# Feed-forward outputs taken from the sum ahead of its layer norm, with mean and factor applied afterwards

## The chip, the cores and the metric

The kernel runs on one core of a Trainium2 chip. The metric is the device time of one execution in microseconds (us), median of the runs shown. TensorE multiplies (PE, and PEld for its weight loads), VectorE (DVE) and ScalarE (ACT) prepare operands and read results, SyncE (SP) issues the loads of weights.

## What is computed

The program runs two transformer blocks; only the end of the second is touched. There the mixer's output is added to the stream and normed, and a gated feed-forward follows (sizes: 256 tokens, D_MODEL 1024, D_FF 2816):

```python
def layer_norm(x, g, b):
    mu = jnp.mean(xf, axis=-1, keepdims=True)
    var = jnp.mean(jnp.square(xf - mu), axis=-1, keepdims=True)
    y = (xf - mu) * lax.rsqrt(var + LN_EPS)
    return (y * g + b).astype(x.dtype)

x = layer_norm(alpha * x + mix, ln1_g[l], ln1_b[l])
ff = (jax.nn.silu(x @ w_ffn_gate) * (x @ w_ffn_up)) @ w_ffn_down
x = layer_norm(alpha * x + ff, ln2_g[l], ln2_b[l])
```

## The kernel before

**Operands.** Everything is fp32 split in two: each operand has a high part (rounded to the matmul's fp32r) and a low part (the rest), and each product is three matmuls, high by high, low by high, high by low. Weights stream in chunks of 128x1024 through a ring of four raw buffers (`raw`, loaded by SP); ScalarE rounds each into `whi` (`highs`), VectorE subtracts to get `wlo` (`lows`), and both of these are rings of five. `highs` and `lows` stand by hand in each engine's program and convert up to 4 (ScalarE) or 3 (VectorE) chunks ahead of the one named.

**Layout.** Activations lie transposed: 8 tiles (`k`) of 128 features by 256 tokens. `XT` holds the stream, `hx` its high and low parts. The first 256 columns of `hx` are the feed-forward's input; the other 256 columns later hold its inner values (`K.fh`, `K.fl`).

**Up to the norm.** Eight outputs `("wo", m)` of 24 matmuls each end the mixer. For each, VectorE adds the stream (`x1`), and VectorE and ScalarE build running sums and squares. The norm itself (`ln1`) takes these steps in turn: eight one-column matmuls sum over partitions (`ln1_sums`, "s1" and "s2"), VectorE makes mean and factor of them and puts them on a diagonal, one matmul each (`ln1_spread`, "m" and "r") spreads them over all partitions, and then, tile by tile, VectorE subtracts the mean (`x1_centre`), multiplies (`x3t`), ScalarE adds the bias and rounds (`x3h`, then `x3`), and VectorE takes the low part (`x3_low`). `keep(n)` puts matmuls on zeros in between, whose results nobody reads.

**Feed-forward.** There are 22 steps `f` (KF); step `f` needs the gate output `("fg", f)`, the up output `("up", f)`, then Silu, the product, its split, and the down matmuls `down(f)` into four held PSUM banks. The first four outputs (fg and up of steps 0 and 1) run side by side in `lin_many`, tile by tile as `x3` comes; later ones run one by one in `lin_wide`. Steps 0 to 3 also carry four groups of transposes of the normed stream (`x3t`), for the residual. `down` of step f-3 stands after the outputs of step f.

**PSUM.** There are eight banks. `Psum.take` gives the bank that was taken longest ago and returns what must have happened to its last holder (`ps.give` says what); TensorE waits for that before the first matmul into it:

```python
        i = min(free, key=lambda i: (max(self.age[i:i + n]), i))
        ...
                out += self.freed.get(self.holder[j], [])
```

**Order on VectorE and ScalarE.** Each is one in-order list. In the feed-forward's loop over `m`, VectorE's first instructions of a step are `lows(("fg", m))` and `lows(("up", m))`, and ScalarE's first is `highs(("fg", m))`. So the chunk of `fg 3` is converted by ScalarE at the start of m = 1, behind the last instruction of m = 0, which is the copy into `K.fh` (L1446), and by VectorE at the same place, behind the subtraction into `K.fl` (L2165).

Of the kernel before, what the change touches and what calls it, by code (L numbers as in the profile page):

```python
# [2482 lines left out]
```

## Time and profile before

| | |
|---|---|
| median of 3 runs | 894.1 us (892.78 to 896.55) |
| profiled execution, its own time | 894.56 us |
| its span in the profile | 892.8 us |
| TensorE busy | 872.5 us, 98% |
| VectorE busy | 627.1 us, 70% |
| ScalarE busy | 440.3 us, 49% |
| TensorE's granted clock, mean | 0.996 |

Matmuls are pipelined, so TensorE counts as busy in small pauses too; the start times of its instructions show where it really stands. Times below are microseconds from the span's start. "x4" after a row means four instructions in it; the bracket at a row's end gives the engine's idle time before it and who ended that.

### The profile page before, as it was taken

How to read it: one execution, taken by the hardware profiler on the slowest of the kernel's cores; microseconds unless marked ns; L12 is line 12 of the kernel's file. 1: busy time of each engine (PE TensorE's matmuls, PEld its weight loads, DVE VectorE, ACT ScalarE, POOL GpSimd, SP SyncE). 2: the span in 40 equal slices, each digit the busy share in tenths (PEclk: the TensorE clock that was granted, in tenths of full speed). 3: DMA queues.
4: the chain of work that ended last, by engine and by line, in shares of the span. 5: the costliest groups of instructions: out<-in, count | busy, mean ns of one | idle time of the engine just before them, and what ended most of it. 6: DMA issues, size and time to landing. Idle time of an engine off the chain costs nothing.

```text
span 892.8 us, 13280 instructions
## 1 busy us (share of the span) xinstructions
PE 872.5 (98%) x5324; PEld 709.2 (79%) x5324; DVE 627.1 (70%) x1252; ACT 440.3 (49%) x750; POOL 21.2 (2%) x16
## 2 busy tenths in 40 slices
PE   8999999999999999999999999999999999999996
PEld 4678477776687777877998888988999888888885
DVE  5532757594836759966699999978688775665666
ACT  3351515543723356555544444566554665555552
POOL 0000000000000000000002121100000000000000
PEclk9999999999999999999999999999999999999999
DMA  9784551100354033203556656441366365546541
GB/s 351 284 319 171 203 197 61 48 25 1 119 196 161 16 130 142 84 23 142 167 189 188 190 173 204 142 143 59 103 196 210 113 201 206 188 175 204 190 164 47
DMA packets 39997, 136.68 MB, mean 153 GB/s; under 512 B 4352, under 2 KB 4480, under 8 KB 39680
## 3 DMA queue, kind: packets, MB, share of 16 engines
q1 hardware_dynamic: 38928, 130.48, 42.8%
q10 hardware_dynamic: 1008, 5.36, 1.6%
q8 instruction: 42, 0.69, 0.3%
q14 instruction: 19, 0.16, 0.1%
HBM read 134.77 MB, written 1.05 MB: 152 GB/s over the span
## 4 chain that ended last, share of the span: by engine, by line
PE 68%; DVE 25%; ACT 3%; DMA 2%; issue 1%; SPq 0%; DVEq 0%; ACTq 0%
PE ps L414 8%; DVE wlo L1472 7%; PE ps L971 6%; DVE AF L1941 6%; PE ps L415 4%; PE ps L369 4%; PE ps L370 4%; PE ps L374 3%; PE ps L733 3%; PE ps L489 3%; PE ps L386 2%; DMA AF<-wmod 2%; PE ps L397 2%; PE ps L756 2%; PE ps L398 2%; PE ps L401 2%
## 5 line engine op out<-in xcount | busy, mean ns | idle before, releaser
L1472 DVE TENSOR_TENSOR wlo<-raw,whi 128x1024 fp32r<-128x1024 f32 (+2 forms) x204 | 231.6, 1158 | 34.4 <-ACT whi L1009 34.2
L1009 ACT ACTIVATE whi<-raw 128x1024 fp32r<-128x1024 f32 (+2 forms) x204 | 203.5, 1005 | 86.2 <-DMA raw<-wpack 45.8
L369 PE MATMUL ps<-hx,whi 128*128 128x256 f32 (+1 forms) x384 | 115.4, 300 | 0.3 <-ACT AF L1350 0.3
L414 PE MATMUL ps<-hx,whi 128*128 128x512 f32 x320 | 113.9, 398 | 0.0
L370 PE MATMUL ps<-hx,whi 128*128 128x256 f32 (+1 forms) x384 | 112.0, 292 | 0.0
L374 PE MATMUL ps<-hx,wlo 128*128 128x256 f32 (+1 forms) x332 | 96.9, 292 | 0.0
L415 PE MATMUL ps<-hx,wlo 128*128 128x256 f32 x320 | 89.8, 281 | 0.0
L369 PEld LDWEIGHTS ps<-hx,whi 128*128 128x128 f32 x384 | 73.3, 191 | 3.8 <-issue 2.3
L370 PEld LDWEIGHTS ps<-hx,whi 128*128 128x128 f32 x384 | 73.4, 191 | 2.0 <-issue 0.7
L459 PE MATMUL ps<-whi,hx 128*128 128x512 f32 (+1 forms) x192 | 71.7, 373 | 0.2 <-ACT acc L1078 0.2
L414 PEld LDWEIGHTS ps<-hx,whi 128*128 128x128 f32 x320 | 60.1, 188 | 14.6
L460 PE MATMUL ps<-wlo,hx 128*128 128x512 f32 (+1 forms) x192 | 70.8, 369 | 0.0
L461 PE MATMUL ps<-whi,hx 128*128 128x512 f32 (+1 forms) x192 | 70.7, 368 | 0.0
L374 PEld LDWEIGHTS ps<-hx,wlo 128*128 128x128 f32 x332 | 63.4, 191 | 1.1
L415 PEld LDWEIGHTS ps<-hx,wlo 128*128 128x128 f32 x320 | 60.4, 189 | 0.7
L1941 DVE SCALAR_TENSOR_TENSOR AF<-AF,cst 128x256 f32<-128x256 f32 x120 | 58.0, 529 | 0.4
L1827 DVE TENSOR_REDUCE AF<-ps 128x1 f32<-128x512 f32 (+1 forms) x48 | 28.7, 598 | 32.1 <-PE ps L733 32.1
L971 PE MATMUL ps<-whi,hx 128*128 128x512 f32 x176 | 50.5, 391 | 0.0
L1240 ACT ACTIVATE AF<-ps 128x512 f32<-128x512 f32 (+1 forms) x48 | 25.0, 523 | 42.9 <-PE ps L741 42.9
L733 PE MATMUL ps<-AF 96*128 96x512 f32 (+1 forms) x96 | 43.1, 530 | 0.4 <-DVE AF L1750 0.4
L1233 ACT ACTIVATE AF<-ps,AF 128x512 f32<-128x512 f32 (+1 forms) x48 | 29.5, 615 | 26.1 <-DVE AF L1827 25.6
L459 PEld LDWEIGHTS ps<-whi,hx 128*128 128x128 f32 x192 | 36.7, 191 | 5.8 <-ACT acc L1078 0.4
(293 smaller groups left out, 1667.2 us busy)
## 6 DMA issues: line engine op xcount, KB each, us to landing
raw<-wpack SPq DMA_DIRECT2D x178, 512.0 KB, 4.1
AF<-wmod SPq DMA_DIRECT2D x48, 512.0 KB, 6.0
raw<-wpack SPq DMA_DIRECT2D x24, 256.0 KB, 2.7
XT<-xin SPq DMA_DIRECT2D x4, 512.0 KB, 6.0
raw<-wpack SPq DMA_DIRECT2D x4, 432.0 KB, 4.9
uq<-wuq ACTq DMA_DIRECT2D x2, 768.0 KB, 5.4
cst<-cpack ACTq DMA_DIRECT2D x1, 1093.0 KB, 8.0
AF<-wukv ACTq DMA_DIRECT2D x2, 512.0 KB, 6.7
```

Of the source, the lines that this page charges most:

```text
L369: e.matmul(o, wh[:, b], xh(k), start=j == 0, stop=False, skip_group_check=True)
L370: e.matmul(o, wh[:, b], xl(k), start=False, stop=False, skip_group_check=True)
L374: e.matmul(o, wl[:, b], xh(k), start=False, stop=False, skip_group_check=True)
L414: e.matmul(ps.ap(key, 512).rearrange("p (s n) -> p s n", s=2), wh[:, b], K.hx[:, :, k, 0:256], start=k == 0, stop=False, skip_group_check= ...
L415: i = e.matmul(ps.ap(key, 256), wl[:, b], hh[:, k, 0:256], start=False, stop=k == KD - 1, skip_group_check=True)
L459: e.matmul(o, xh(k)[:, ts], wh[:, b], start=k == 0, stop=False, skip_group_check=True)
L460: e.matmul(o, xh(k)[:, ts], wl[:, b], start=False, stop=False, skip_group_check=True)
L461: i = e.matmul(o, xl(k)[:, ts], wh[:, b], start=False, stop=k == KD - 1, skip_group_check=True)
L971: i = e.matmul(ps.ap(("fd", t), 512, 512 * q), y[:, f % 8, x], w[:, 512 * q:512 * q + 512], start=f == 0 and y is K.fh and w is wh, stop=f ...
L1009: e.activation(W.hi(i), W.raw(i), ACT.Copy).then_inc(*HI.up(j))
L1472: e.tensor_tensor(W.lo(i), W.raw(i), W.hi(i), ALU.subtract).then_inc(*LO.up(j))
L1941: e.scalar_tensor_tensor(out=g.CV[:, m, :], in0=g.U[:, m, j:j + 256], scalar=w, in1=g.CV[:, m, :], op0=ALU.mult, op1=ALU.add).then_inc(*V. ...
```

## The change

The six outputs of steps 0, 1 and 2 (RAW = 3) no longer read the normed input. Their input is `K.rx`: the sum ahead of the norm times the norm's weight, as high and low parts, in the columns 256 to 511 of `hx`; two more columns (256 wide becomes 258) hold the norm's weight and bias themselves. So each output comes with two extra numbers per partition, by which VectorE turns it into what the normed input would have given: copy the two numbers, (mean row x first number + output), times the factor row, and the bias number enters in Silu's bias or in the product. The sums and spreads of the norm now stand between the matmuls of `lin_raw`, and the matmuls on zeros are gone. Mean and factor rows are copied out of PSUM by ScalarE. The normed stream is still made as before, for steps 3 and up and for the residual; the four groups of transposes move from steps 0 to 3 to steps 3 to 6.

```diff
@@ tensor_program
-    keep(1)
-    ln1_sums("s1", K.acc[:, 0:256], K.XT[:, 7, XC], V["x1sum", 6], V["x1", 7])
-    ln1_sums("s2", K.acc[:, 256:512], K.sq[:, 768:1024], V["sqadd", 6], A["x1sq", 7])
-    ln1_spread("m", 256)
-    keep(2)
-    ln1_spread("r", 0)
-    keep(2)
+    rh, rl, rw = (lambda k: K.rx[:, 0, k, :]), (lambda k: K.rx[:, 1, k, :]), (lambda k: V["xr", k])
...
+    def lin_raw(specs):
+        got = []
+        for key, wname, cols in specs:
+            free = ps.take(key)
+            got.append((weights(key, (wname, 0, tuple(range(KD)), cols), KD * P), free))
+        for k in range(KD):
+            b = slice(k * P, (k + 1) * P)
+            pe.wait_ge(A["gb"], A["xr", k], V["gb"], V["xr", k])
+            for (key, wname, cols), ((c, wh, wl), free) in zip(specs, got):
...
+            if k == 0:
+                ln1_sums("s1", K.acc[:, 0:256], K.XT[:, 7, XC], V["x1sum", 6], V["x1", 7])
+                ln1_sums("s2", K.acc[:, 256:512], K.sq[:, 768:1024], V["sqadd", 6], A["x1sq", 7])
+            if k == 1:
+                ln1_spread("m", 256)
+            if k == 2:
+                ln1_spread("r", 0)
@@ for f in range(KF)
-            lin_many([((nm, j), f"w_ffn_{w}_2", 0, (P * j, P), x2h, x2l, 256) for j in range(2) for nm, w in (("fg", "gate"), ("up", "up"))], lambda k: A["x3h", k], xt3)
-        elif f > 1:
-            lin_wide(("fg", f), "w_ffn_gate_2", cc, xt3)
-            lin_wide(("up", f), "w_ffn_up_2", cc, xt3)
-        if f < 4:
+            lin_raw([((nm, j), f"w_ffn_{w}_2", (P * j, P)) for j in range(2) for nm, w in (("fg", "gate"), ("up", "up"))])
+        elif 1 < f < RAW:
+            lin(("fg", f), "w_ffn_gate_2", 0, cc, range(KD), rh, rl, 258, rw)
+            lin(("up", f), "w_ffn_up_2", 0, cc, range(KD), rh, rl, 258, rw)
+        elif f >= RAW:
+            lin_wide(("fg", f), "w_ffn_gate_2", cc, xt3, ps.bank.get(("ln1", "s2")) if f == RAW else None)
+            lin_wide(("up", f), "w_ffn_up_2", cc, xt3, ps.bank.get(("ln1", "m")) if f == RAW else None)
+        if RAW <= f < RAW + 4:
@@ scalar_program
+    def raw_high(m):
+        ac.wait_ge(V["x1", m])
+        e.activation(K.rx[:, 0, m, 0:256], XT[:, m, XC], ACT.Copy, scale=C("l1g", m, 1)).then_inc(*A.up(("xr", m)))
...
+    highs(("up", 1), 1)
+    for what, z in (("m", 0), ("r", 256)):
+        ac.wait_ge(M["ln1", what])
+        e.activation(K.acc[:, z:z + 256], ps.ap(("ln1", what), 256), ACT.Copy).then_inc(*A.up(("ln1", what)))
...
+        if k == 4:
+            highs(("up", 1), 2)
...
-        ac.wait_ge(V["fu", m], M["fd", m - 8, 1] if m >= 8 else None)
+        ac.wait_ge(V["fu", m], M["fd", m - 8, 1] if m >= 8 else M["up", RAW - 1])
         e.activation(K.fh[:, m % 8, :], K.AF[:, 512 + z:768 + z], ACT.Copy).then_inc(*A.up(("f", m)))
@@ vector_program
+    def raw_low(m):
+        dv.wait_ge(A["xr", m])
+        e.scalar_tensor_tensor(out=K.rx[:, 1, m, 0:256], in0=XT[:, m, XC], scalar=C("l1g", m, 1), in1=K.rx[:, 0, m, 0:256], op0=ALU.mult, op1=ALU.subtract).then_inc(*V.up(("xr", m)))
...
     diagonal("r", 0, v)
+    lows(("up", 1), 1)
+    for m in range(5, 8):
+        raw_low(m)
     for k in range(2):
         x1_centre(k)
...
+        if k == 5:
+            lows(("up", 1), 2)
     x3_low(KD - 1)
-    lows(("up", 1), 1)
+    def normed(nm, m, y, dst):
+        sc = K.modrow[:, 4 * m + 2 * y:4 * m + 2 * y + 2]
+        dv.wait_ge(M[nm, m])
+        e.tensor_copy(sc, ps.ap((nm, m), 2, 256)).then_inc(*V.up())
+        dv.wait_ge(V.now(), A["ln1", "r"])
+        e.scalar_tensor_tensor(out=dst, in0=K.acc[:, 0:256], scalar=sc[:, 0:1], in1=ps.ap((nm, m), 256), op0=ALU.mult, op1=ALU.add).then_inc(*V.up())
+        ps.give((nm, m), V.now())
+        dv.wait_ge(V.now())
+        e.tensor_tensor(dst, dst, K.acc[:, 256:512], ALU.mult).then_inc(*V.up((nm + "n", m)))
...
+        if m < RAW:
+            normed("fg", m, 0, side[:, 0:256])
+            normed("up", m, 1, side[:, 256:512])
+            dv.wait_ge(A["fg", m], V.now())
+            e.scalar_tensor_tensor(out=h, in0=side[:, 256:512], scalar=K.modrow[:, 4 * m + 3:4 * m + 4], in1=K.AF[:, z:z + 256], op0=ALU.add, op1=ALU.mult).then_inc(*V.up(("fu", m)))
```

**Order on TensorE, where the mixer's last output ends.** Before, the sums (L943), the spreads (L948) and the matmuls on zeros (L524) stand here, and the first matmul of `lin_many` (L430) behind them:

```order
L372 MATMUL ps<-hx,wlo 128x256
L524 MATMUL ps<-zero 128x256 [waits dve_done]
L943 MATMUL ps<-cst,acc 128x1 [waits dve_done]
...
L943 MATMUL ps<-cst,wk 128x1
L948 MATMUL ps<-wk,cst 128x256 [waits dve_done]
L524 MATMUL ps<-zero 128x256 x2
L948 MATMUL ps<-wk,cst 128x256 [waits dve_done]
L524 MATMUL ps<-zero 128x256 x2
L430 MATMUL ps<-hx,whi 128x256 [waits w_low,act_done]
```

With the change, the place of the first filler is taken by `lin_raw`: L967 to L969 are its three matmuls for one tile and one output, L945 the sums, which stand behind twelve of them (the first of those, the last two and the sums are shown).

```order
L374 MATMUL ps<-hx,wlo 128x256
L967 MATMUL ps<-hx,whi 128x258 [waits w_low,act_done,dve_done]
...
L968 MATMUL ps<-hx,wlo 128x258
L969 MATMUL ps<-hx,whi 128x258
L945 MATMUL ps<-cst,acc 128x1 [waits dve_done]
L945 MATMUL ps<-cst,acc 128x1
...
L945 MATMUL ps<-cst,wk 128x1
L967 MATMUL ps<-hx,whi 128x258
```

So the sums moved behind the first tile of the four outputs, and nothing on zeros is left.

**Order on TensorE, fifth and sixth output.** These are the last matmuls of `lin_raw` and the first of `("fg", 2)`, L371, which is in `lin`:

```order
L968 MATMUL ps<-hx,wlo 128x258
L969 MATMUL ps<-hx,whi 128x258
L371 MATMUL ps<-hx,whi 128x258 [waits dve_done,w_low]
L372 MATMUL ps<-hx,whi 128x258
L376 MATMUL ps<-hx,wlo 128x258
```

L371 waits for VectorE as well as for its weights. Eight banks were taken since `("fg", 0)` took its own (four outputs, s1, s2, m, r), so `("fg", 2)` takes the bank of `("fg", 0)`, and what frees it is the second operation of `normed` for that output (L2201).

**Order on VectorE, end of the norm and step 0 of the feed-forward, before.** L2131 is `x3_low`, L2136 `x3t`, L1472 `lows`, L2153 the product of step 0, L2165 the low part of its result:

```order
L2136 SCALAR_TENSOR_TENSOR wk<-XT,cst,ps 128x256 [waits dve_done]
L2131 SCALAR_TENSOR_TENSOR hx<-wk,cst,hx 128x256 [waits act_done] x2
L1472 TENSOR_TENSOR wlo<-raw,whi 128x1024 [waits w_high]
L2153 TENSOR_TENSOR AF<-AF,ps 128x256 [waits act_done,mm_done]
L2165 TENSOR_TENSOR hx<-AF,hx 128x256 [waits act_done]
L1472 TENSOR_TENSOR wlo<-raw,whi 128x1024 [waits w_high] x2
```

And now, where L2186 is `x3t`, L2181 `x3_low`, L2199, L2201 and L2204 are `normed`, L2216 the product, L2227 the low part, L1511 `lows` (the last row is the chunk of fg 3):

```order
L2186 SCALAR_TENSOR_TENSOR wk<-XT,cst,acc 128x256 [waits dve_done]
L2181 SCALAR_TENSOR_TENSOR hx<-wk,cst,hx 128x256 [waits act_done] x2
L2199 COPY modrow<-ps 128x2 [waits mm_done]
L2201 SCALAR_TENSOR_TENSOR AF<-acc,modrow,ps 128x256 [waits dve_done]
L2204 TENSOR_TENSOR AF<-AF,acc 128x256 [waits dve_done]
L2199 COPY modrow<-ps 128x2 [waits mm_done]
L2201 SCALAR_TENSOR_TENSOR AF<-acc,modrow,ps 128x256 [waits dve_done]
L2204 TENSOR_TENSOR AF<-AF,acc 128x256 [waits dve_done]
L2216 SCALAR_TENSOR_TENSOR AF<-AF,modrow 128x256 [waits dve_done,act_done]
L2227 TENSOR_TENSOR hx<-AF,hx 128x256 [waits act_done]
L1511 TENSOR_TENSOR wlo<-raw,whi 128x1024 [waits w_high]
```

`normed` came in behind the last `x3_low`, and the conversion for fg 3 stands behind all of step 0.

**Order on ScalarE, from the norm's end to the chunk of fg 3, with the change.** L1457 is `x3`, L1475 Silu, L1485 the copy into `K.fh`, L1034 `highs`:

```order
L1462 ACTIVATE hx<-wk,cst 128x256 [waits dve_done]
L1457 ACTIVATE XT<-wk,cst 128x256 x2
L1475 ACT_TABLE_LOAD
L1475 ACTIVATE AF<-AF,modrow 128x256 [waits dve_done]
L1485 ACTIVATE hx<-AF 128x256 [waits mm_done,dve_done]
L1034 ACTIVATE whi<-raw 128x1024 [waits raw_in0]
```

L1485 waits for TensorE too, for the end of `("up", 2)`, because `K.fh` lies where the matmuls of steps 0 to 2 read. The conversion for fg 3 stands behind it.

## Rows read from the trace of the kernel before

**Rows 1.** The page: busy time, share of the span and instructions.

```profile
PE 872.5 (98%) x5324; PEld 709.2 (79%) x5324; DVE 627.1 (70%) x1252; ACT 440.3 (49%) x750; POOL 21.2 (2%) x16
```

**Rows 2.** Windows: length, PE, PEld, DVE, ACT, POOL busy (count), clock, DMA, GB/s.

```profile
691.40:697.87 6.47, 5.36 (x33) 4.30 (x32) 5.19 (x21) 0.93 (x2) 0.00 (x0) 1.00 0.67 246
697.87:709.30 11.43, 11.40 (x95) 11.43 (x96) 8.76 (x22) 9.59 (x19) 0.00 (x0) 1.00 0.04 5
725.00:733.40 8.40, 8.40 (x46) 7.17 (x45) 5.66 (x10) 5.35 (x10) 0.00 (x0) 1.00 0.62 213
```

**Rows 3.** Timeline, TensorE around the norm: start us, us, engine line.

```profile
691.53 0.59 PE L524 MATMUL ps<-zero 128*128 128x256 f32 x2
693.18 0.53 PEld L943 LDWEIGHTS ps<-cst,wk 128*128 128x128 f32 x4
693.63 0.30 PEld L948 LDWEIGHTS ps<-wk,cst 128*128 128x128 f32 x2
693.96 0.84 PEld L524 LDWEIGHTS ps<-zero 128*128 128x128 f32 x4
697.90 0.36 PE L430 MATMUL ps<-hx,whi 128*128 128x256 f32 x1 [0.34 <-ACT hx L1424]
```

**Rows 4.** Timeline of VectorE at the end of the mixer's output.

```profile
690.17 1.22 DVE L1472 TENSOR_TENSOR wlo<-raw,whi 128x1024 fp32r<-128x1024 f32 x1
691.73 0.42 DVE L2097 SCALAR_TENSOR_TENSOR XT<-XT,ps 128x256 f32<-128x256 f32 x1 [0.33 <-PE ps L372]
```

**Rows 5.** Timeline of VectorE in the norm.

```profile
693.94 0.16 DVE L2121 SCALAR_TENSOR_TENSOR nrm<-ps,nrm 128x2 f32<-128x2 f32 x1
695.85 0.75 DVE L2111 TENSOR_TENSOR XT<-XT,ps 128x256 f32<-128x256 f32 x2
696.73 0.48 DVE L2136 SCALAR_TENSOR_TENSOR wk<-XT,cst,ps 128x256 f32<-128x256 f32 x1
703.05 0.47 DVE L2136 SCALAR_TENSOR_TENSOR wk<-XT,cst,ps 128x256 f32<-128x256 f32 x1
704.91 0.48 DVE L2131 SCALAR_TENSOR_TENSOR hx<-wk,cst,hx 128x256 fp32r<-128x256 f32 x1 [0.20 <-ACT hx L1424]
```

**Rows 6.** Timeline of ScalarE in the norm.

```profile
701.74 0.50 ACT L1419 ACTIVATE XT<-wk,cst 128x256 f32<-128x256 f32 x1
```

**Rows 7.** Timeline of a feed-forward step, VectorE.

```profile
718.97 0.42 DVE L2163 TENSOR_TENSOR AF<-AF 128x256 f32<-128x256 f32 x1
719.88 0.42 DVE L2165 TENSOR_TENSOR hx<-AF,hx 128x256 fp32r<-128x256 f32 x1 [0.48 <-ACT hx L1446]
720.22 2.35 DVE L1472 TENSOR_TENSOR wlo<-raw,whi 128x1024 fp32r<-128x1024 f32 x2
```

**Rows 8.** Timeline of the same step, ScalarE.

```profile
719.43 0.42 ACT L1446 ACTIVATE hx<-AF 128x256 fp32r<-128x256 f32 x1 [0.94 <-DVE AF L2163]
719.75 0.58 ACT L1450 ACTIVATE AF<-ps 128x512 f32<-128x512 f32 x1
720.23 1.05 ACT L1009 ACTIVATE whi<-raw 128x1024 fp32r<-128x1024 f32 x1
```

**Rows 9.** Timeline, TensorE's weight loads at steps 3 to 5.

```profile
721.89 0.48 PEld L988 LDWEIGHTS ps<-cst,XT 128*128 128x128 f32 x4
722.34 0.30 PEld L971 LDWEIGHTS ps<-whi,hx 128*128 128x128 f32 x2
724.96 0.19 PEld L414 LDWEIGHTS ps<-hx,whi 128*128 128x128 f32 x1
733.35 0.19 PEld L414 LDWEIGHTS ps<-hx,whi 128*128 128x128 f32 x1
```

**Rows 10.** Windows, same columns: after one-column matmuls, and at the end.

```profile
84.00:86.00 2.00, 2.00 (x9) 2.00 (x10) 1.20 (x8) 0.00 (x0) 0.00 (x0) 0.50 0.00 0
86.00:88.00 2.00, 2.00 (x12) 2.00 (x12) 0.21 (x2) 0.00 (x0) 0.00 (x0) 0.66 0.00 0
888.00:890.00 2.00, 0.00 (x0) 0.00 (x0) 1.82 (x7) 0.00 (x0) 0.00 (x0) 0.87 0.00 0
```

More of the change, by code:

```diff
@@ L286 @@
 ITEMS2 = [(qb, h) for qb in range(2) for h in range(8)]
+RAW = 3
 LAST = KF - 4
@@ L404, in lin_rest, with lin_wide @@
         ps.drop(key)
-    def lin_wide(key, wname, cols, xw):
-        free = ps.take(key)
+    def lin_wide(key, wname, cols, xw, at=None):
+        free = ps.take(key, at=at)
         c, wh, wl = weights(key, (wname, 0, tuple(range(KD)), cols), KD * P)
@@ L948, in ln1_spread @@
         e.matmul(ps.ap(("ln1", what), 256), C("ones"), K.rs[:, z:z + 256], start=True, stop=True, skip_group_check=True).then_inc(*M.up(("ln1", what)))
-    keep(1)
-    ln1_sums("s1", K.acc[:, 0:256], K.XT[:, 7, XC], V["x1sum", 6], V["x1", 7])
-    ln1_sums("s2", K.acc[:, 256:512], K.sq[:, 768:1024], V["sqadd", 6], A["x1sq", 7])
-    ln1_spread("m", 256)
-    keep(2)
-    ln1_spread("r", 0)
-    keep(2)
-    xt3 = lambda k: V["x3", k]
+    rh, rl, rw = (lambda k: K.rx[:, 0, k, :]), (lambda k: K.rx[:, 1, k, :]), (lambda k: V["xr", k])
+    xt3 = lambda k: V["x3", k]
+    def lin_raw(specs):
[7 more added lines that the diff above has]
+            for (key, wname, cols), ((c, wh, wl), free) in zip(specs, got):
+                o = ps.ap(key, 258)
+                pe.wait_ge(*free)
+                e.matmul(o, wh[:, b], rh(k), start=k == 0, stop=False, skip_group_check=True)
+                e.matmul(o, wl[:, b], rh(k), start=False, stop=False, skip_group_check=True)
+                i = e.matmul(o, wh[:, b], rl(k), start=False, stop=k == KD - 1, skip_group_check=True)
+                if k == KD - 1:
+                    i.then_inc(*M.up(key))
+                    W.given[c] = M.now()
+            if k == 0:
[5 more added lines that the diff above has]
+                ln1_spread("r", 0)
     def down(f, ts):
@@ L1414, in scalar_program @@
         e.activation(K.sq[:, z:z + 256], XT[:, m, XC], ACT.Square).then_inc(*A.up(("x1sq", m)))
+    raw_high(7)
     e.dma_start(K.AF[:, 3072:5120], K.l2rows).then_inc(*K.l2_in.up("rows"))
+    highs(("up", 1), 1)
+    for what, z in (("m", 0), ("r", 256)):
+        ac.wait_ge(M["ln1", what])
+        e.activation(K.acc[:, z:z + 256], ps.ap(("ln1", what), 256), ACT.Copy).then_inc(*A.up(("ln1", what)))
+        ps.give(("ln1", what), A.now())
     def x3(k):
@@ L2109, in x1_centre @@
     def x1_centre(k):
-        dv.wait_ge(M["ln1", "m"])
-        e.tensor_tensor(XT[:, k, XC], XT[:, k, XC], ps.ap(("ln1", "m"), 256), ALU.add).then_inc(*V.up(("x1c", k)))
+        dv.wait_ge(A["ln1", "m"])
+        e.tensor_tensor(XT[:, k, XC], XT[:, k, XC], K.acc[:, 0:256], ALU.add).then_inc(*V.up(("x1c", k)))
     dv.wait_ge(M["ln1", "s1"])
@@ L2171, in vector_program @@
         x, y = g.x3t[:, t, :], g.yt[:, t, :]
-        dv.wait_ge(M["fd", KF - 1, t], A["x3t", 2 * t + 1])
+        dv.wait_ge(M["fd", KF - 1, t], A["x3t", RAW + 2 * t + 1])
         e.tensor_tensor_reduce(x, ps.ap(("fd", t), D), x, 1.0, 0.0, ALU.add, ALU.add, nm).then_inc(*V.up())
@@ L2277, in build @@
         K.mean = K.acc[:, 256:512]
-        K.x1 = [K.AF[:, 9216 + 256 * i:9472 + 256 * i] for i in range(4)]
         K.mod = sb("mod", [P, 96])
```

35 lines of the change are left out of this document (18 added, 17 removed).

## Prediction

> **What bounds the kernel now.** I read the page first: TensorE is busy 98% of the span [rows 1], so what it cannot issue is what time is lost, and other engines matter where it waits for them. Then the windows. In the norm, 691.40 to 697.87, TensorE's share looks high only because sums and matmuls on zeros count as work [rows 2]. In the timeline the last useful matmul is followed at 691.53 by a filler, and the first feed-forward matmul starts at 697.90 [rows 3]: 6.4 us in which nothing but the norm's eight sums and two spreads is issued. After that TensorE runs without a pause: 96 matmuls in 11.43 us [rows 2], 0.12 us each, and in a full step 8.40 us of 8.40 are busy, while VectorE has 5.66 us of work and ScalarE 5.35 [rows 2]. So before, the norm costs one hole, and behind it both helpers have room.
>
> **What the change removes.** The hole. Call T the start of the first raw matmul. The chunk it needs last is converted by 691.39 [rows 4], and VectorE, which gets a raw low part (0.39 us of its time) in each mixer output, had 0.33 us idle in it [rows 4]; five of them put it up to 0.3 us late. I take T = 691.6. Twelve matmuls of 258 columns for each tile: two columns more in 256 is 1%, so I keep 0.12 us, 1.45 us for a tile. The sums keep their cost: a group of four loads takes 0.45 us (693.18 to 693.63 [rows 3]), four groups 1.8; a spread takes 0.33 (693.63 to 693.96 [rows 3]), two 0.7. TensorE alone would end the four outputs at 691.6 + 11.6 + 1.8 + 0.7 = 705.7, and `fg 2` and `up 2` (24 matmuls each, 5.8 us) at 711.5. Before, this much work was done at 716.3 less the first two groups of transposes (0.9 us): on TensorE alone the gain is about 4 us.
>
> **What it adds on VectorE's path.** Now follow the norm itself. The second sum starts its last group at T + 1.45 + 1.35 = 694.4; the variance (L2121) follows 0.76 us behind that start (693.18 to 693.94 [rows 3, 5]), so at 695.15. The factor takes what it took, 1.91 us from there to the next free slot (693.94 to 695.85 [rows 5]): 697.05, 1.2 us later than before. Into that slot the change puts a low part of weights (1.17 us, half of the pair's 2.35 [rows 7]) and three raw low parts (1.17); then the two centrings (0.7 with the start of the next). The first `x3t` starts at 700.1, where it started at 696.73 [rows 5]. The tile chain took 8.18 us from there to the last `x3_low` (704.91 [rows 5]). At its sixth tile one more low part of weights stands, behind a ScalarE conversion of 1.05 us [rows 8] that follows `x3(3)` (end 702.24 [rows 6]): 702.24 + 1.05 + 1.17 = 704.4 where the next `x3t` stood at 703.05 [rows 5], 1.36 us. Its own wait, for the end of `fg 0`, is over by then (704.9 against 705.5 on the new clock). So the last `x3_low` starts at 700.1 + 8.2 + 1.35 = 709.65. ScalarE's copies of mean and factor lie beside this: the second spread starts at 698.1, and `x3t` asks for its copy 2 us later.
>
> **First stall.** Only behind that does VectorE come to `normed` of `fg 0`: copy at 710.05, the sum with the mean row at 710.25, done 710.75 (0.48 as L2136 with its pointer [rows 5]; the copy priced by the 0.2 us spacing of small operations, which fits 693.94 to 695.85: nine starts). `fg 2` waits for it, since it takes that bank. TensorE is free at 705.7: it stands 5.1 us.
>
> **Second stall.** `fg 2` and `up 2` run 710.8 to 716.6. ScalarE's copy into `K.fh` waits for their end: 716.8. Behind it stands the conversion for `fg 3`: 0.32 us later it starts (719.43 to 719.75 [rows 8]), takes 1.05 [rows 8]; VectorE's low part takes 1.22 more [rows 4]. `fg 3` starts at 719.45: 2.9 us of waiting. VectorE's work of step 0 (the product, 2.6 us behind 709.65) and ScalarE's table load lie under the run of `fg 2`.
>
> **Third stall, and the rest.** The low part for `up 3` stands behind step 1 on VectorE: two `normed` (1.1 us each), the product (0.45), 0.45 for ScalarE's copy (718.97 to 719.43 [rows 7, 8]), 0.45 to the low part (719.88 [rows 7]), 0.34 to the weights (720.22 [rows 7]), 1.2: 4.6 us behind `fg 3`'s start. An output takes 2.88 us (733.35 - 724.96 for two and a `down`, which takes 724.96 - 722.34 = 2.62 [rows 9]), so TensorE waits 1.7 us, then does `up 3`, transposes (0.45, 721.89 to 722.34 [rows 9]) and `down(0)`. Step 2 on VectorE ends the low part for `fg 4` 10.4 us behind `fg 3`'s start, when TensorE is at 10.55: no wait. Then 2.88 twice, 0.45 and 2.62: `fg 5` starts 19.4 us behind 719.45, at 738.85. Before it started at 733.35 [rows 9]: 5.5 us later, with two groups of transposes still to come, 0.9. From there VectorE and ScalarE have room as before, and the tail keeps its length.
>
> **The clock.** TensorE stands 5.1 us with no fillers. In this trace it came out of one-column matmuls at 84 with a clock of 0.50, then 0.66 over the next stretch [rows 10]: about 3.4 us at the lower level, 1.2 GHz, worth at most 1.7 us of work. After the last matmul it was still high for some 5 us and fell within 888 to 890 (mean 0.87 [rows 10]). Both happened, then: low after thin work, high for some time after none. I take a fall inside the first stall, part of it paid while nothing runs: 1.3 us, between 0 and 1.7. A second fall at `fg 3` would be hidden by the third stall. The Trainium skill, TensorE: Matmul & The Clock Gate, section Why this matters for your kernels, asks for no pauses between bursts of matmuls, since the array comes back at half rate. It speaks against a change that trades fillers for a stall. By that rule the result is 901.8, without a fall 900.5.
>
> **Sum.** 5.5 + 0.9 + 1.3 = 7.7 us. On the profiled execution's own 894.56 us that is 902.3, on the median of 894.1 it is 901.8, and that is my figure.
>
> **The rivals.**
> The stalls without the clock: 900.5 us, 20%.
> The chain is shorter than its rows: mean and factor now come from SBUF and not from PSUM, T is earlier, `normed` is quicker. If it ends 2.5 us earlier, 899; 12%. Little speaks for it: an operation of this form takes 0.48 us from SBUF (L2131) and 0.47 to 0.48 from PSUM (L2136) [rows 5]. The two-column copy, which no row shows, lies between the 0.16 us of a two-column operation and the 0.48 of a full one [rows 5]; at the upper end the first stall is 0.3 us longer.
> The clock falls again at `fg 3` and lasts into `up 3`, or stays low over all of `fg 2` and `up 2`: 2 to 3 us more, 904.5; 8%.
> Faster: the outputs' PSUM banks come free in time. It decides at 705.7: were `normed` of `fg 0` done by then, and the chunk of `fg 3` converted by 711.5, the 4 us gain would stand, 890.1 us. That needs VectorE 5 us ahead of its rows, or a bank that I have named wrongly; 3%.
> The forecast itself has 57%. Its own range is 900.8 to 903.2, by T (0.5 us) and the clock (0 to 1.7). The range over the cases takes in the shorter chain and the second fall: 898 to 905. Half a per cent, 4.5 us, is about what a measurement of this kernel tells from no change: slower by over that (above 898.6) are the forecast, the clockless case, the longer fall and two thirds of the shorter chain, 0.9 in all; within it 0.07; faster 0.03.
>
> **What the profile will show.** L967 follows the last `("wo", 7)` matmul within 0.3 us; sums and spreads stand between without waiting. L371's first matmul waits some 5 us for VectorE's L2201; the first L416 (`fg 3`) some 3 us for L1511, and the next some 1.7 us. The granted clock has 0.5 behind the first wait. From step 5 on the step is 8.3 us again. I am wrong if the first of these waits is under 3 us, which would mean that VectorE's chain starts or runs faster; if L371 names another waker; or if a later step waits too (weights late, since each raw buffer is freed by a later low part), which would add to the time.

## The result, and the profile after

| | before | after |
|---|---|---|
| median (5 runs each) | 894.1 us (892.78 to 896.55) | 909.15 us (906.82 to 910.4) |
| profiled execution: its own time, span | 894.56, 892.8 us | 909.83, 908.0 us |
| TensorE's granted clock, mean | 0.996 | 0.989 |

The ratio is 1.016, 95% interval 1.0136 to 1.0183: 15 us slower, twice what the prediction summed. The page's first part, for [rows 1]:

```profile
PE 880.0 (97%) x5330; PEld 712.7 (78%) x5330; DVE 635.6 (70%) x1277; ACT 443.4 (49%) x759; POOL 21.2 (2%) x16
```

TensorE waits at the first two places where it was said to. Its waits from 690 to 760 us (waited for: us in total, times, longest):

```profile
PE ps L371 <- DVE AF L2201: 4.8, 1, 4.8
PE ps L416 <- DVE wlo L1511: 2.8, 1, 2.8
```

VectorE, from the timeline: the last sum `x1` (L2142), the variance (L2168), the low part that went in ahead of the tile chain, the first `x3t`, the last `x3_low`, `normed` of `fg 0`, and the end of step 0:

```profile
696.89 0.42 DVE L2142 SCALAR_TENSOR_TENSOR XT<-XT,ps 128x256 f32<-128x256 f32 x1
700.46 0.16 DVE L2168 SCALAR_TENSOR_TENSOR nrm<-ps,nrm 128x2 f32<-128x2 f32 x1
702.37 1.22 DVE L1511 TENSOR_TENSOR wlo<-raw,whi 128x1024 fp32r<-128x1024 f32 x1
705.37 0.48 DVE L2186 SCALAR_TENSOR_TENSOR wk<-XT,cst,acc 128x256 f32<-128x256 f32 x1
714.88 0.48 DVE L2181 SCALAR_TENSOR_TENSOR hx<-wk,cst,hx 128x256 fp32r<-128x256 f32 x1 [0.19 <-ACT hx L1462]
715.47 0.48 DVE L2201 SCALAR_TENSOR_TENSOR AF<-acc,modrow,ps 128x256 f32<-128x256 f32 x1
724.81 0.43 DVE L2227 TENSOR_TENSOR hx<-AF,hx 128x256 fp32r<-128x256 f32 x1 [6.76 <-ACT hx L1485]
725.76 1.22 DVE L1511 TENSOR_TENSOR wlo<-raw,whi 128x1024 fp32r<-128x1024 f32 x1 [0.52 <-ACT whi L1034]
```

Subtract 5.16 from each (691.73 in [rows 4] is 696.89 here) and the forecast chain stands there: first `x3t` 700.2 (forecast 700.1), last `x3_low` 709.7 (709.65). But that subtraction is the first surprise: at 696.89 TensorE has issued no instruction yet that the change adds or moves.

ScalarE, timeline of the second stall: its copy into `K.fh` waits 6.89 us for the end of `up 2`, and the conversion for `fg 3` stands behind the copy:

```profile
724.37 0.42 ACT L1485 ACTIVATE hx<-AF 128x256 fp32r<-128x256 f32 x1 [6.89 <-PE ps L374]
724.69 1.04 ACT L1034 ACTIVATE whi<-raw 128x1024 fp32r<-128x1024 f32 x1
```

TensorE's weight loads, timeline: first of `fg 2`, last of `up 2`, first of `fg 3`, `up 3`, `fg 4` and `fg 5` (for [rows 9]):

```profile
716.07 0.29 PEld L371 LDWEIGHTS ps<-hx,whi 128*128 128x128 f32 x1 [4.93 <-issue]
...
723.87 0.19 PEld L374 LDWEIGHTS ps<-hx,wlo 128*128 128x128 f32 x1
727.04 0.19 PEld L416 LDWEIGHTS ps<-hx,whi 128*128 128x128 f32 x1 [2.98 <-DVE wlo L1511]
...
731.76 0.19 PEld L416 LDWEIGHTS ps<-hx,whi 128*128 128x128 f32 x1 [0.42 <-DVE wlo L1511]
...
737.71 0.19 PEld L416 LDWEIGHTS ps<-hx,whi 128*128 128x128 f32 x1
...
746.57 0.19 PEld L416 LDWEIGHTS ps<-hx,whi 128*128 128x128 f32 x1
```

Windows over the first stall and behind it (columns as in [rows 2]; the clock is the third number from the end):

```profile
711.20:714.00 2.80, 0.15 (x2) 0.00 (x0) 2.73 (x6) 1.91 (x5) 0.00 (x0) 1.00 0.01 3
714.00:716.00 2.00, 0.00 (x0) 0.00 (x0) 1.74 (x6) 1.98 (x6) 0.00 (x0) 0.53 0.74 254
716.00:720.90 4.90, 4.80 (x22) 4.83 (x23) 1.88 (x5) 1.46 (x2) 0.00 (x0) 0.50 0.03 8
720.90:724.30 3.40, 3.37 (x28) 3.16 (x26) 0.00 (x0) 0.00 (x0) 0.00 (x0) 0.99 0.00 0
```

The clock fell to 1.2 GHz just behind 714, 1.9 us before the stall ended (a mean of 0.53 from 714 to 716), and stayed there for 4.9 us of matmuls: `fg 2` and `up 2` took 8.0 us, 716.07 to about 724.0, where 5.8 were summed. It fell a second time behind the second stall, where `fg 3` runs:

```profile
728.00:731.00 3.00, 3.00 (x11) 2.52 (x11) 2.34 (x7) 2.76 (x4) 0.00 (x0) 0.50 0.54 171
```

**Where the 15.2 us between the two profiled executions lie**, by starts of the same instruction in both (a reduction on VectorE at 140 us, the last `x1`, the first weight load of `lin_wide` in steps 5, 8 and 21, the end):

| stretch | before | after | more |
|---|---|---|---|
| start to the reduction | 140.20 | 141.41 | 1.2 |
| to the last `x1` | 551.53 | 555.48 | 3.95 |
| to `fg 5` | 41.62 | 49.68 | 8.06 |
| to `fg 8` | 25.15 | 26.28 | 1.13 |
| to `fg 21` | 109.03 | 109.79 | 0.76 |
| to the end | 25.27 | 25.36 | 0.1 |

The two rows that begin the second stretch, timeline of VectorE, kernel before:

```profile
140.20 0.42 DVE L1827 TENSOR_REDUCE AF<-ps 128x1 f32<-128x256 f32 x1
```

and after:

```profile
141.41 0.42 DVE L1866 TENSOR_REDUCE AF<-ps 128x1 f32<-128x256 f32 x1
```

The 8.06 and 0.9 of the 1.13 are what the forecast was about. The rest lies where TensorE's instructions are the same: 1.2 at the start, a stretch that varies from 138.9 to 142.1 us between executions with this same layout, and 3.95 + 0.23 + 0.76 = 4.9 us over all the rest. (Of the 3.95, 0.2 can belong to the change: VectorE makes five raw low parts in the last outputs of the mixer, and e1 below, which has the layout alone, shows 3.7.) The groups of matmuls by line and shape (0 to 690 us: busy us, mean ns) are 1 to 1.5% longer there. Before:

```profile
L459 PE MATMUL ps<-whi,hx 128*128 128x512 f32 x144 | 56.6, 393 | 0.0
L460 PE MATMUL ps<-wlo,hx 128*128 128x512 f32 x144 | 56.1, 390 | 0.0
```

After:

```profile
L461 PE MATMUL ps<-whi,hx 128*128 128x512 f32 x144 | 57.4, 399 | 0.0
L462 PE MATMUL ps<-wlo,hx 128*128 128x512 f32 x144 | 56.7, 394 | 0.0
```

Ends of matmuls are modelled, so starts must say it too: a `down` of twelve such matmuls (stationary operand in `hx`, moving one in `whi` or `wlo`) takes 2.633 us from first load to the next output's before, 2.673 after (means over steps 8 to 21), and a step 8.386 and 8.449 us (means of the last eight).

### The profile page after: what moved, and what is told of

Its sections match the earlier page's. It is cut to its first block, busy times and chain, and to the rows that moved or that the text cites. A ratio compares the mean times of both kernels' runs of the same rounds, so it can differ in the third digit from the quotient of the medians.

```text
span 908.0 us, 13333 instructions
## 1 busy us (share of the span) xinstructions
PE 880.0 (97%) x5330; PEld 712.7 (78%) x5330; DVE 635.6 (70%) x1277; ACT 443.4 (49%) x759; POOL 21.2 (2%) x16
## 4 chain that ended last, share of the span: by engine, by line
PE 80%; DVE 12%; ACT 3%; DMA 2%; issue 1%; SPq 0%; DVEq 0%; ACTq 0%
PE ps L416 8%; PE ps L993 6%; PE ps L371 5%; PE ps L372 5%; PE ps L461 5%; PE ps L463 4%; PE ps L462 4%; PE ps L376 4%; PE ps L417 4%; PE ps L735 3%; PE ps L491 3%; DVE wlo L1511 2%; DMA AF<-wmod 2%; PE ps L399 2%; PE ps L388 2%; PE ps L758 2%
## 5 line engine op out<-in xcount | busy, mean ns | idle before, releaser
L1511 DVE TENSOR_TENSOR wlo<-raw,whi 128x1024 fp32r<-128x1024 f32 (+2 forms) x204 | 231.8, 1159 | 35.8 <-ACT whi L1034 35.7
L1034 ACT ACTIVATE whi<-raw 128x1024 fp32r<-128x1024 f32 (+2 forms) x204 | 203.2, 1005 | 86.2 <-DMA raw<-wpack 41.6
L371 PE MATMUL ps<-hx,whi 128*128 128x256 f32 (+2 forms) x400 | 121.1, 303 | 5.1 <-DVE AF L2201 4.8
L372 PE MATMUL ps<-hx,whi 128*128 128x256 f32 (+2 forms) x400 | 117.3, 293 | 0.0
L416 PE MATMUL ps<-hx,whi 128*128 128x512 f32 x304 | 110.0, 401 | 2.9 <-DVE wlo L1511 2.8
L376 PE MATMUL ps<-hx,wlo 128*128 128x256 f32 (+2 forms) x346 | 102.0, 295 | 0.0
L417 PE MATMUL ps<-hx,wlo 128*128 128x256 f32 x304 | 86.5, 285 | 0.0
L371 PEld LDWEIGHTS ps<-hx,whi 128*128 128x128 f32 x400 | 76.6, 192 | 9.2 <-issue 7.2
L372 PEld LDWEIGHTS ps<-hx,whi 128*128 128x128 f32 x400 | 76.8, 192 | 2.2 <-issue 0.7
L461 PE MATMUL ps<-whi,hx 128*128 128x512 f32 (+1 forms) x192 | 72.7, 379 | 0.2 <-ACT acc L1103 0.2
L463 PE MATMUL ps<-whi,hx 128*128 128x512 f32 (+1 forms) x192 | 71.8, 374 | 0.0
L416 PEld LDWEIGHTS ps<-hx,whi 128*128 128x128 f32 x304 | 58.1, 191 | 17.4 <-DVE wlo L1511 3.4
```

Of the source, the lines that this page charges most:

```text
L371: e.matmul(o, wh[:, b], xh(k), start=j == 0, stop=False, skip_group_check=True)
L372: e.matmul(o, wh[:, b], xl(k), start=False, stop=False, skip_group_check=True)
L376: e.matmul(o, wl[:, b], xh(k), start=False, stop=False, skip_group_check=True)
L416: e.matmul(ps.ap(key, 512).rearrange("p (s n) -> p s n", s=2), wh[:, b], K.hx[:, :, k, 0:256], start=k == 0, stop=False, skip_group_check= ...
L417: i = e.matmul(ps.ap(key, 256), wl[:, b], hh[:, k, 0:256], start=False, stop=k == KD - 1, skip_group_check=True)
L461: e.matmul(o, xh(k)[:, ts], wh[:, b], start=k == 0, stop=False, skip_group_check=True)
```

## The experiments

Each run's 4 to 12 executions stood beside executions of the kernel before on the same chip. The ratio compares the two sets as wholes, so it is not quite the quotient of their medians (e1: 899.0 beside 894.83). "140 to x1" is the second stretch of the table above (551.53 before, 555.48 after), "step" the mean of the last eight steps (8.386 before, 8.449 after), good to 0.002.

| run | median us | ratio (95%) | 140 to x1 | step |
|---|---|---|---|---|
| e1: before, stride 514 | 899.0 | 1.0056 (1.0043 to 1.0069) | 555.3 | 8.449 |
| e2: before, 128 B behind hx | 898.05 | 1.0042 (1.0029 to 1.0054) | 554.2 | 8.390 |
| e3: after, stride 528 | 904.02 | 1.0107 (1.0091 to 1.0122) | 553.2 | 8.351 |
| e4: after, banks | 902.38 | 1.0088 (1.0075 to 1.0102) | 555.0 | 8.449 |
| e5: before, 128 B ahead of AF | 894.47 | 1.0005 (0.9994 to 1.0016) | 551.6 | 8.386 |
| e6: before, 128 B ahead of hx | 894.9 | 1.001 (1.0001 to 1.0019) | 551.7 | 8.386 |
| e7: after, both stalls | 903.28 | 1.0111 (1.0095 to 1.0126) | 555.2 | 8.449 |
| e8: after, 40 fillers | 919.22 | 1.0289 (1.0275 to 1.0303) | 555.2 | 8.449 |
| e9: after, 11 fillers | 907.35 | 1.0143 (1.013 to 1.0157) | 555.2 | 8.447 |
| e10: e7, second down's chunk | 900.55 | 1.0072 (1.006 to 1.0084) | 555.2 | 8.449 |
| e11: e10, rings at 34816 | 898.23 | 1.0044 (1.0032 to 1.0056) | 554.4 | 8.406 |
| e12: before, 2048 B behind hx | 894.26 | 0.9998 (0.9988 to 1.0007) | 551.6 | 8.388 |
| e13: e10, fg 3 earlier, stride 528 | 895.63 | 1.0016 (1.0003 to 1.0028) | 553.1 | 8.351 |
| e14: before, stride 528, rings at 34816 | 894.72 | 1.001 (0.9998 to 1.0023) | 553.1 | 8.353 |
| e15: before, 1024 B behind hx | 894.31 | 1.0001 (0.9988 to 1.0014) | 551.7 | 8.388 |
| e16: before, 512 B behind hx | 894.17 | 1.0001 (0.9991 to 1.0012) | 551.6 | 8.386 |
| e17: e13, copies on ScalarE | 894.32 | 0.9994 (0.9985 to 1.0004) | 553.3 | 8.353 |
| e18: e17, stride 520 | 896.0 | 1.0012 (1.0001 to 1.0022) | 554.0 | 8.394 |

### The loss ahead of the changed place

SBUF of the kernel before, in bytes of a partition from `hx`'s start: `hx` 0 to 32768 (16 tiles of 2048), `raw` from 32768, `whi` from 49152, `wlo` from 69632, `AF` behind. The change makes each tile 2056 bytes and shifts all that follows by 128.

**e1.** The stride alone:

```diff
-        K.hx = sb("hx", [P, 2, KD, TT], F32R)
+        hx = sb("hx", [P, 2, KD, TT + 2], F32R)
+        K.hx = hx[:, :, :, 0:TT]
```

> The kernel before with one edit: the rows of hx are 514 elements apart and not 512, as the change made them; the two extra columns are not used. The trace after is 5.2 us late already at the last output of the mixer, ahead of anything that the change does there, and 0.06 us a step is lost again in steps 8 to 21. Theory A (the odd row stride makes TensorE's reads of hx, or of what lies behind it, slower): 5.2 + 1 = about 6 us slower than before, ratio 1.006 to 1.008, and the last x1 of the second block at about 697 where it was 691.7. Theory B (the loss comes from elsewhere, as from the place of code or from the state of the chip in those executions): no difference, ratio 0.999 to 1.001.

0.56% slower, 5 us, with the last `x1` at 696.55, where it waits 0.33 us for TensorE just as before. The declaration of a buffer makes a third of the change's price. Theory B falls.

```profile
696.55 0.42 DVE L2097 SCALAR_TENSOR_TENSOR XT<-XT,ps 128x256 f32<-128x256 f32 x1 [0.33 <-PE ps L372]
```

**e2.** `+        K.pad = sb("pad", [P, 32])` behind `hx`:

> The kernel before with one edit: 32 unused elements behind hx, whose stride stays 512, so that all later tensors lie 128 bytes higher, just as in the changed kernel. Theory A (the stride of hx itself): no difference. Theory A2 (the place of the weights' rings and the rest, shifted by 128 bytes): about 6 us slower, ratio 1.006 to 1.008. Theory B: no difference here and none in the run with stride 514.

Theory A in its plain form falls: with `hx` untouched, 128 bytes behind it cost 0.42%, 3.8 us. (Its trace has 2.7 of them between 140 us and the last `x1` and none in the steps, where `down` takes 2.671 us for 2.633, but the two outputs 5.720 for 5.753.) **e5** and **e6** put the same pad elsewhere.

> The kernel before with 128 unused bytes between wlo and AF: hx and the three weight rings (raw, whi, wlo) stay where they were, AF, wk, acc and the small tensors lie 128 bytes higher. The pad behind hx cost 3.8 us (0.42%). If the place of the rings makes that cost: no difference here (ratio 0.999 to 1.001). If the place of AF and what follows it makes it: 1.004.

> The kernel before with 128 unused bytes between XT and hx: hx, the rings and all that follows lie 128 bytes higher, and hx and the rings keep their distance. If the distance between hx (the stationary operand of the 512-column matmuls that got slower) and the rings (their moving operand) decides: no difference. If the rings' own address decides: 1.004, as with the pad behind hx.

Ahead of `AF` it costs nothing, so the rings matter. Ahead of `hx` everything moves, and 0.1% is left (0.9 us, of which the two columns on the right show 0.2); so it isn't mainly the rings' own address but how they lie to `hx`. **e12, e15 and e16** widen the pad behind `hx`.

> The kernel before with 2048 unused bytes behind hx instead of 128. A pad of 128 cost 0.42%, the same pad ahead of hx 0.1%, ahead of AF nothing, so the distance between hx and the rings decides. If it is the distance modulo 2048 bytes or less, in which all tiles and all ring slots are alike before: no difference, ratio 0.999 to 1.001. If it is a coarser address or the exact distance: up to 1.004.

> The kernel before with 1024 unused bytes behind hx. 128 bytes cost 0.42%, 2048 nothing. If the rule is a multiple of 2048 (a full 512-column row), this costs about 0.4%; if a multiple of 1024 or less, nothing.

> The kernel before with 512 unused bytes behind hx. If the rule is a multiple of 512 (the 128 columns of a stationary tile) or less, nothing; if 1024 or 2048, about 0.4%.

2048, 1024 and 512 bytes cost nothing, 128 cost 0.42%. Whether 256 costs was not run. **e3 and e14** take the stride to 528 elements, 2112 bytes, with the rings 33792 and 34816 bytes behind `hx`'s start, both multiples of 512.

> The changed kernel with one edit: rows of hx 528 elements apart instead of 514, so each tile starts at a multiple of 64 bytes again. Theory A with alignment as its cause: 6 us faster than the changed kernel, about 903, ratio to before 1.009 to 1.011. Theory A with any stride but 512 as its cause, or theory A2 (the later tensors' place): stays at 909. The two stalls (4.9 us before fg 2, 3.0 before fg 3) stay as they are under all of them.

> The kernel before with tiles of hx 528 elements apart and the rings 34816 bytes behind hx's start. If only the rings' distance from the start of hx counts, no difference (ratio 0.999 to 1.001); if each tile's own distance counts, as the 2.9 us suggest that stayed with 514 and the rings at this place, 1.002 to 1.004.

In the changed kernel it gives back 5.1 us of the 15; in the kernel before it costs 0.1%, with both signs inside: 1.5 us lost up to `x1`, and 0.035 us gained in each step, in which `down` is slower (2.656 for 2.633) and the two outputs faster (5.695 for 5.753).

The same two signs show between 140 us and the last `x1`, if the time from each matmul's start to the next one's is summed by form. There are 838 matmuls of 512 columns with an operand in `hx`, and 1512 of 256 columns. The first take 3.65 us more in e1 than before, and still 3.2 us more in e14; the second take 0.1 us more in e1 and 1.8 us less in e14. So tiles 64 bytes off do not give the 512-column matmuls their pace back: they make the 256-column ones faster, which covers the loss. The groups of e14 say the same (L369, 256 columns, took 291 ns before; L459 and L460 took 393 and 390):

```profile
L369 PE MATMUL ps<-hx,whi 128*128 128x256 f32 x344 | 99.4, 289 | 0.3 <-ACT AF L1350 0.3
L459 PE MATMUL ps<-whi,hx 128*128 128x512 f32 x144 | 57.3, 398 | 0.0
L460 PE MATMUL ps<-wlo,hx 128*128 128x512 f32 x144 | 56.5, 393 | 0.0
```

### The two stalls

**e4.** Only the PSUM banks of `fg 2` and `up 2`:

```diff
-            lin(("fg", f), "w_ffn_gate_2", 0, cc, range(KD), rh, rl, 258, rw)
-            lin(("up", f), "w_ffn_up_2", 0, cc, range(KD), rh, rl, 258, rw)
+            lin(("fg", f), ..., rw, ps.bank.get(("ln1", "s1")))
+            lin(("up", f), ..., rw, ps.bank.get(("ln1", "r")))
```

> The changed kernel with one edit: fg 2 and up 2 take the PSUM banks of s1 and r, which are free by then, instead of those of fg 0 and up 0. No instruction moves. My account of the first stall: it goes (4.9 us), and so does its fall of the clock (2.4 us of slow work). The second stall stays in part: product of step 0 at 718.0, copy into K.fh 0.4, then 2.7 us as now from that copy to fg 3, which starts at 720.7 where it was 727.0: 6.3 us faster than the changed kernel, 902.5 to 903.5, with a wait of 3.8 us for VectorE's L1511. Rival 1 (the chain through VectorE decides anyway, the stall only moves to fg 3): under 2 us faster, 907 or more. Rival 2 (without the waits all is well): 894 or less.

6.8 us faster than after, and one wait is left, 3.6 us where 3.8 were forecast. The timeline of TensorE in e4, at `fg 3`:

```profile
719.43 0.72 PE L416 MATMUL ps<-hx,whi 128*128 128x512 f32 x1 [3.65 <-DVE wlo L1511]
```

Its last `x1` is at 695.55, so `fg 3` stands 23.9 us behind it; in the changed kernel 727.04 - 696.89 = 30.15. The bank's price is 6.3 us, as forecast: 4.9 of standing, 2.0 of slow clock (e8 below), less the 0.7 by which the second wait is longer (3.65 for 2.98). Behind that wait the clock falls here too; windows of e4:

```profile
716.00:719.00 3.00, 0.00 (x0) 0.00 (x0) 1.89 (x4) 1.51 (x3) 0.00 (x0) 1.00 0.00 0
720.00:722.00 2.00, 2.00 (x8) 1.71 (x7) 1.83 (x5) 1.46 (x2) 0.00 (x0) 0.50 0.60 197
```

**e8 and e9** price the clock alone: `keep`'s matmuls on zeros in the first stall, in the free bank of `s1`.

```diff
         elif 1 < f < RAW:
+            pe.wait_ge(*ps.freed.get(("ln1", "s1"), []))
+            for _ in range(40):        # e9: 11
+                e.matmul(ps.ap(("ln1", "s1"), 256), K.zero[:, 0:P], K.zero[:, :], ...)
```

> The changed kernel with 40 matmuls on zeros (0.12 us each, 4.8 us) ahead of fg 2, in the bank of s1: they lie in the first stall, whose end is set by VectorE. The clock's part: it was low for 4.9 us of matmuls behind that stall. If it stays high, fg 2 and up 2 take 5.8 us and not 8.3: 2.4 us faster than the changed kernel, 906 to 907.3. If the clock costs nothing in the end (the next wait takes it up): no difference.

> The changed kernel with 11 matmuls on zeros ahead of fg 2, in the bank of s1. The run with 40 showed that one of them takes 0.43 us, not 0.12 (they are plain fp32), so that they ran 12 us past the stall; 11 take 4.7 us and fill it. With the clock high, fg 2 and up 2 take 5.8 us, as they did in that run, where they took 8.2 in the changed kernel: 2.4 us faster than the changed kernel, 906 to 907.5, if the clock's price stands to the end; no difference if the next wait takes it up.

e8 failed by my arithmetic: one filler is plain fp32 and takes 0.43 us (40 from 711.46 to 728.63), which [rows 3] would have told (the four loads of two fillers take 0.84 us). But `fg 2` and `up 2` behind it, at a clock of 1.00, took 5.76 us from first load to last (728.63 to 734.39), for 7.80 in the changed kernel (716.07 to 723.87): the slow clock cost 2.0 us. e9 fits the stall: windows of e9,

```profile
711.00:716.00 5.00, 4.99 (x25) 4.09 (x24) 4.68 (x11) 4.09 (x9) 0.00 (x0) 1.00 0.37 107
716.00:722.00 6.00, 5.94 (x48) 5.73 (x48) 1.69 (x5) 1.27 (x2) 0.00 (x0) 1.00 0.00 1
722.00:726.00 4.00, 1.29 (x4) 1.11 (x5) 2.89 (x7) 1.63 (x3) 0.00 (x0) 0.84 0.13 16
```

and it is 1.8 us faster by the medians, 2.3 by the two spans (905.7, 908.0). The clock's fall costs about 2 us (both expectations said 2.4), and the second stall does not hide it, since ScalarE's copy waits for the end of `up 2`.

**e7 and e10** attack the second and third stall as well. Banks and transposes lie as the expectation says, ScalarE converts the same chunks earlier too, and VectorE has this in place of the loop's first three rounds (`lows` with the last chunk that it converts):

```diff
+    lows(("up", 1), 3)            # fg 3, right behind the last x3_low
+    normed("fg", 0, ...)
+    lows(("fg", 2), 3)            # up 3
+    normed("up", 0, ...); product(0)
+    normed("fg", 1, ...); inner_low(0)
+    lows(("up", 2), 3)            # the first down
+    normed("up", 1, ...); product(1)
+    normed("fg", 2, ...)
+    lows(("fg", 3), 3)            # fg 4
+    inner_low(1); normed("up", 2, ...)
+    lows(("up", 3), 3)            # up 4
+    product(2); inner_low(2)
+    lows(("fd", 0), 3)            # the second down: e10 only
```

> The changed kernel with both stalls attacked. Banks: fg 1 and up 1 in 6 and 7, fg 2 in that of s1, up 2 in that of s2, fg 3 and up 3 in those of m and r, transposes at steps 4 to 7, so nothing on TensorE waits for normed before fg 4. Conversions: the chunk of fg 3 right behind the last x3_low, those of up 3, the first down, fg 4 and up 4 between the operations of steps 0 to 2. My theory that the order alone made the loss: fg 3 starts at 716.9 (trace of after's clock) where it was 727.0, with no wait; VectorE has 14.2 us of work from 715.45 that up 4 needs, so 1.2 us of waits at fg 4 and up 4; in the end 10 to 11 us faster than the changed kernel, 898 to 899.5; still above before because the slower matmuls (about 5 us) stay. Rival (VectorE has too much to do in steps 0 to 2, whatever the order): waits of 3 us or more at fg 4 to fg 5, 901 or more.

> The version that attacks both stalls, with one more conversion moved: the chunk of the second down is converted by VectorE right behind step 2, and not behind step 3. In its trace TensorE waited 2.4 us there (down(1), for L1513), and 0.4, 0.8 and 0.8 at earlier places. Order is all that is missing: the 2.4 us go, 898 in the execution that then took 900.4, a median of 900 to 901 (the other three executions of that version took 903.3). If VectorE has too much to do: the wait comes back one place later, no difference.

e7 is 5.9 us faster than after, and missed 898 to 899.5. Its time is what the rival had (901 or more), but not by the rival's waits: those at `fg 3` and `fg 4` were 0.8 us each, and one of 2.4 us stood at the second `down`, which I had not followed so far. e10 takes it away by order alone (900.55 for 903.28, as expected). In e10 the waits of TensorE from 690 to 790 us are

```profile
PE ps L417 <- DVE wlo L1513: 2.3, 3, 0.8
PE ps L994 <- DVE wlo L1513: 0.4, 1, 0.4
```

2.7 us, where 1.2 were summed. They stand at `fg 3`, `fg 4`, `fg 5` and the first `down`. The first is ScalarE's: VectorE idled 1.26 us behind the last `x3_low` for its conversion of `fg 3`. **e11, e13, e17, e18** go on from there. e11 moves the rings only:

> The version of the run beside it (both stalls attacked, one more conversion moved) with 1920 unused bytes behind hx, so that the rings start 34816 bytes behind hx's start, a multiple of 2048 again as in the kernel before, while the tiles of hx stay 514 elements apart. If the distance of the rings from the start of hx is what counts: the 512-column matmuls are back at 390 ns and it is 4 to 5 us faster than that version. If each tile's own distance counts (tile k is 8k bytes off): up to 1 us.

2.3 us faster, between the two forecasts: by the total, about half of the 5 us is the rings' shift, the rest goes with each tile's own offset (tile k lies 8k bytes off). But the 512-column group did not come back to 390 ns, as the first forecast had it (397 and 394 in e11's trace), and `down` took 2.682 us for e10's 2.673; what got faster is the two outputs (5.724 for 5.773) and the 256-column matmuls.

e13 lets ScalarE convert `fg 3` at `k == 5` of the tile chain, and takes stride 528:

> The version with both stalls attacked and the second down's chunk moved, with two more edits: ScalarE converts the chunk of fg 3 inside the tile chain (ahead of x3h(6), where it stood idle 0.9 us) instead of behind it, so VectorE's low part follows the last x3_low without its 1.3 us of idling; and hx's tiles are 528 elements apart with the rings 34816 bytes behind hx's start. Order: the wait at fg 3 (0.8) goes, and the later ones (0.4, 0.8, 0.7) shrink by 0.5 each: 1.9 to 2.3 us less than 900.5. Placement: if tiles 64 bytes off cost less than tiles 8 bytes off, another 2 to 4 us: 894.5 to 896.5 in all; if only the order helps: 898.

895.63, in the forecast range; two edits made it, and no run parts them. From the last `x1` to `fg 5` it needs 40.0 us and has three transposes (1.35) to come, 41.35, for 41.62 with none before: the first version in which the feed-forward's start is no slower.

e17 moves six copies, `e.tensor_copy(sc, ...)` on VectorE, to ScalarE (`e.activation(sc, ..., ACT.Copy)`):

> The version with both stalls attacked and stride 528, with one more edit: the six copies of two columns (the norm's weight and bias numbers of each output) are made by ScalarE, four behind the last x3 and two behind Silu of step 0. In that version's trace TensorE still waited 0.8 us at fg 4 and 0.8 at up 4 for VectorE's L1515, 0.2 at the first down. If VectorE's amount of work makes these waits: 5 copies of 0.18 us fewer ahead of fg 4, 0.9 us, so both waits nearly go: 1.2 to 1.6 us less than 895.6, that is 894 to 894.5, no longer to be told from before. If the order or ScalarE makes them: no difference, 895.6.

> The same as the run beside it with hx's tiles 520 elements apart and not 528 (each tile 32 bytes further off a multiple of 512, not 64), the rings still 34816 bytes behind hx's start. If the price falls with each doubling of the offset (8 bytes about 4 us with the rings in place, 64 bytes 1 us): 0.5 to 1.5 us slower than the run beside it. If all that counts is 64 or not 64: 2 us or more slower. If the offset doesn't matter from 32 on: the same.

The waits of e17 in the same stretch are half of e13's 1.8:

```profile
PE ps L417 <- DVE wlo L1525: 1.0, 2, 0.8
```

So VectorE's amount of work made the one at `fg 4` (0.8, now 0.25); the other, which stood at `fg 5` and not at `up 4` as the expectation has it, stays at 0.8. e17 and before can't be told apart (0.9994); it is 1.6% faster than the changed kernel. From the last `x1` to `fg 8`, with all transposes done in both, it takes 65.2 us for 66.8 before, so the change does gain 1.6 us there, and the 1.7 us lost up to the last `x1` (553.3 for 551.5) take them back. A tile 32 bytes off (e18) costs 1.7 us more than 64.

## Why the prediction was wrong

It said 901.8, 898 to 905; 909.15 came. By its own steps:

- **T and TensorE's work.** Right but for the offset: from the last `x1` to the end of `lin_raw` it forecast 14.0 us (691.73 to 705.7), and the last load stands 14.1 behind it in after (710.95).
- **VectorE's chain.** Right to 0.2 us in each mark, once 5.16 is subtracted (variance 695.3 for 695.15, last `x3_low` 709.72 for 709.65).
- **First stall.** Forecast 5.1 us, came 4.9; e4 shows that the bank of `fg 0` is its cause.
- **Second and third.** Forecast 2.9 and 1.7. `fg 3` waited 3.0, and `up 3` started 4.7 us behind it (forecast 4.6), but the clock fell a second time, so the loads show only 0.42 idle there: slow matmuls ran into time that was lost anyway. That a second fall would be hidden by the third stall was right; the rival, in which it lasts into `up 3`, did not come. The terms listed for the 4.6 add up to 5.1, since the product's 0.45 lies inside the stretch from 718.97 to 719.43 that prices ScalarE's copy; with it counted once they give the 4.6.
- **The clock.** The term was mis-sized: 1.3, between 0 and 1.7; it was 2.0 (7.80 us for e8's 5.76), and e9 gives 1.8 to 2.3 back. I took 3.4 us of low clock from [rows 10] and assumed that part of it would pass while nothing runs. Part did, 1.9 us before the stall ended, but the clock was low for 6.8 us in all, and the 4.9 behind the stall were all paid. The Trainium skill, TensorE: Matmul & The Clock Gate, section Why this matters for your kernels, asks for no long pauses between bursts of matmuls, since the clock goes back to half. The traces agree: it fell in the stall of 4.9 us, and in e9, where fillers stood in the stall's place, it stayed at 1.00 up to 722 us, past `fg 2` and `up 2`.
- **Sum of these:** 8.06 + 0.9 for the two later transposes, 9.0 for a forecast of 7.7. That alone would be 903.1 us, inside the range.
- **The step that failed is a term put at nothing without a reason.** The start from T = 691.6 and "From there VectorE and ScalarE have room as before, and the tail keeps its length" took for granted that code which the diff does not touch runs as it ran. The diff has a line that touches it: `hx` grew from 512 to 514 columns. By the two traces 3.95 + 0.23 + 0.76 = 4.9 us stand there; e1, the layout alone, measures 5.0 (3.8 to 6.2), and e3 takes 5.1 back. With the 9.0 above and the 1.2 of the first stretch that is 15.1. No rival had it, so the range could not hold the time.

Open: why the distance counts. What is shown is that 128 bytes cost and 512, 1024 and 2048 don't, and that with stride 514 the 512-column matmuls with an operand in `hx` get slower, by 3 to 6 ns each from start to start where `hx` holds the stationary one (229.3 to 235.0 ns for the 288 with a moving operand in `whi`). With 528 they stay slow and the 256-column ones get 1 ns faster. What makes either, and whether other engines' accesses take part, no run separates. Open too is what moves the first 140 us: with the layout of after it took 138.9 to 142.1 us in six executions, so the 1.2 us there can't be given to the change.

## What to carry to other kernels

A buffer's size in a diff is part of the change: list what reads it or lies behind it, over the whole program, and try the declaration alone. Where a pool hands out banks in turn, an output whose reader moved late blocks the one that comes a round later; naming another free bank was worth 6.8 us in two lines. Shifting work from a full engine's hole to a helper's chain gains only if the helper has the time: of 4 us that TensorE could gain here, banks, the order of the helpers' lists and what stood on which helper decided between 9 us lost and 1.6 gained.
